# A feed-forward stage in seven block products, with the down product as a stage of its own

## The chip, the core and the metric

The kernel runs on one core of a Trainium2 chip. Times are device microseconds of one execution; the profile shows one execution more closely. Engines: PE (TensorE, matmuls), PEld (its weight loads), DVE (VectorE), ACT (ScalarE), POOL (GpSimd), and SP (SyncE), whose queue issues all DMAs here. Each engine runs its own instruction list in order; they wait for each other through semaphores.

## What is computed

Two transformer blocks on a sequence of 1024 rows of width 1024, all in float32. The part that is changed is the feed-forward layer of the first block (D_FF = 2816 = 22 x 128):

```
h2 = rms_norm(x, g_ffn[layer])
x = x + (jax.nn.silu(h2 @ w_ffn_gate[layer]) * (h2 @ w_ffn_up[layer])) @ w_ffn_down[layer]
```

The second block needs modulation vectors (shift, scale, gate), products of one activated row `c` with `ada_w_2` and `kv_ada_w_2`, 8192 columns in all: 64 pieces of 512 KB. They are computed beside the feed-forward layer.

## The kernel before, in words

Activations lie transposed: a tile holds 128 channels on the partitions and the 1024 rows of the sequence in the free dimension, in two halves (h = 0, 1) of 512. A float32 product is made of three fp32r matmuls: each operand is split in a high part and a low part (value minus high part), and high x high, high x low, low x high are summed in PSUM.

Weights come in units of 512 KB (128 x 1024 in SBUF). For each unit SP loads `raw` (`sp_w`), ACT makes the high part `wh` (`act_w`, L73), POOL the low part `wl` (`pool_w`, L76), PE uses it (`gemm`, L67). There are three places each for raw, high and low. `act_w(e, key, ahead)` is called at a fixed point of each engine's list and does all units up to so many past `key`.

The work runs as stages: attention and gates of the first block, branches, output product `out` (`pe_out`, by halves, with the squares and sums of the norm `n2`), feed-forward (`*_ffn`), a join with the last group of the down product (`*_join`), then the second block.

In the feed-forward stage hidden tile f (128 of 2816 columns) is a gate product `("fg", f)` and an up product `("fu", f)` on the tiles `bh`, `bl` (the scaled and split h2), 48 matmuls each. ACT takes silu of the gate, DVE multiplies by the up product (`hid`), ACT and POOL split the result in `G` (`gh`, `gl`), which holds five tiles. After each group of hidden tiles (GROUPS: 2, 4, 4, 4, 4, 4) `pe_down` adds the group before to the residual `X`: 8 products, DVE adds each to X. The last group is left to the join. The entry of the stage, `pe_first_two`, does half 0 of two products while the sums, root and scaling of half 1 are made.

The modulation runs between: per piece a DMA into `ada`, a DVE product and a DVE reduction (L106), and after every fourth piece four small matmuls. PSUM is four banks of 1024 columns, taken in turn (`take`).

Of the kernel before, what the change touches and what calls it, by code (L numbers as in the profile page):

```python
# [119 lines left out]
class Bank:  # L120


    def __init__(self, ap):
        self.ap, self.before = ap, []
# [12 lines left out]
class Net:  # L137
    def __init__(self, nc, A, C, out, mem, known, dry):
        self.nc, self.A, self.C, self.out, self.mem, self.dry = nc, A, C, out, mem, dry
        self.table, self.places, self.plan, self.unit_no = known  # L140
        self.sig = {}
        self.units = 0
# [29 lines left out]
    def setup(self):  # L172
        self.raw = [self.sb(f"raw{i}", i) for i in range(3)]
        self.wh = [self.sb(f"wh{i}", 3 + i, dt=FR) for i in range(3)]
        self.wl = [self.sb(f"wl{i}", 6 + i, dt=FR) for i in range(3)]
# [3 lines left out]
        self.banks = [Bank(t[:, :]) for t in self.mem["ps"]]  # L179
# [49 lines left out]
        self.X = [m(f"X{j}", 8 + j) for j in range(NT)]  # L229
        self.mh = [m(f"mh{j}", 16 + j, FR) for j in range(8)]  # L230
# [5 lines left out]
        self.ada = [m("ada0", 1), m("ada1", 7)]  # L236
        self.acc4 = self.sb("acc4", 51, 512)
# [18 lines left out]
        self.xs = self.dram("xs", [S, S])  # L256
        self.qd = self.dram("qd", [2048, S])
# [4 lines left out]
        self.n2 = five("n2", self.X)  # L262
        self.n3 = Norm("n3", self.X, t[0], t[1], half(t[3]), half(self.dg2), half(t[4]), t[2], self.v(V_GFIN))
        self.n4 = five("n4", self.X)
        self.n5 = five("n5", self.Y)

# [14 lines left out]
    def take(self, e, key, ring=None):  # L281
        ring = self.banks if ring is None else ring
        bank = ring.pop(0)
        ring.append(bank)
        for before in bank.before:
            e.wait_ge(*self.at("free", before))
        bank.before = [key]
        self.places[key] = bank.ap
        return bank.ap
# [4 lines left out]
    def part_banks(self):  # L294
        kept = self.banks.pop(0)
        self.kept = kept
        self.po = [Bank(kept.ap[:, 0:512]), Bank(kept.ap[:, 512:1024])]
        for x in self.po:
            x.before = list(kept.before)

    def join_banks(self):
        self.kept.before = self.po[0].before + self.po[1].before
        self.banks.insert(0, self.kept)
# [7 lines left out]
    def unit(self, key, w8):  # L311
        u = self.units
        self.units += 1
        if self.dry:
            self.plan.append(w8)
            self.unit_no[key] = u
        return u

    def upto(self, key, ahead):
        return min(self.unit_no[key] + ahead, len(self.plan)) if key is not None else ahead  # L320

    def sp_w(self, e, key, ahead=4):

        while self.n_sp < self.upto(key, ahead):
            u = self.n_sp
            src, nk, n = self.plan[u]
            if u >= 3:
                e.wait_ge(*self.at("whi", u - 3))
                e.wait_ge(*self.at("wlo", u - 3))
            e.dma_start(self.raw[u % 3][:, 0:nk * n].rearrange("p (k n) -> p k n", k=nk), src).then_inc(  # L330
                self.sig[f"raw{u % 3}"].up(("raw", u)), 16)
            self.n_sp += 1

    def act_w(self, e, key, ahead=3):
# [2171 lines left out]
```

## Time and profile before

| | us |
|---|---|
| median of 3 runs | 2804.19 |
| lowest, highest | 2799.44, 2804.88 |
| the profiled execution's own time | 2798.98 |
| its span, first to last instruction | 2797.4 |
| mean granted clock of TensorE | 0.976 of full speed |

The page gives for each engine the time in which it is busy; its slices and the windows show stretches. A wait of an engine is named by the instruction that ended it. The time of the profiled execution is its span and 1.6 us around it.

### The profile page before, as it was taken

The page shows a single profiled execution, that of the slowest core. Times are in us where ns is not written, and L with a number is a line of the kernel's source. Part 1 is how long each engine was busy: PE and PEld are TensorE (multiplying, and loading weights), DVE is VectorE, ACT ScalarE, POOL GpSimd, SP SyncE. Part 2 cuts the span into 40 slices and gives each one's busy share as a digit, 9 for nine tenths or more (in the row PEclk, how much of TensorE's full clock was granted, in tenths as well). Part 3 has the DMA queues.
Part 4 walks back from the last instruction along what each step waited for, and adds up shares of the span by engine and source line. Part 5 has one row for each costly group of instructions (what it writes and reads, how often), then busy time and mean ns, then how long its engine had stood idle before and what let it go on. Part 6 is the DMA issues. An engine that isn't in the chain of part 4 may idle for free. (4 is left out here: it accounts for less than half of the span.)

```text
span 2797.4 us, 30789 instructions
## 1 busy us (share of the span) xinstructions
PE 2647.7 (95%) x12448; PEld 2195.2 (78%) x12448; DVE 1420.0 (51%) x2330; ACT 858.6 (31%) x1307; POOL 941.0 (34%) x443
## 2 busy tenths in 40 slices
PE   5999999889998999999999978999999988999888
PEld 4888888678786888888888757888888866788877
DVE  5599999597425536364541273121313256007943
ACT  4432112477223211111111253212121245227732
POOL 2147422100544432333232334333242344323333
PEclk8999999999999999999999989999999989999999
DMA  4112233000542324343331111111111123332142
GB/s 159 43 38 61 91 91 99 26 1 31 181 136 76 113 75 121 106 121 99 112 105 51 48 53 46 45 50 41 50 48 45 53 68 106 121 104 67 50 143 98
DMA packets 292569, 221.78 MB, mean 79 GB/s; under 512 B 8425, under 2 KB 275149, under 8 KB 292429
## 3 DMA queue, kind: packets, MB, share of 16 engines
q1 hardware_dynamic: 292428, 219.82, 25.6%
q8 instruction: 99, 1.62, 0.2%
q14 instruction: 42, 0.34, 0.0%
HBM read 187.25 MB, written 31.49 MB: 78 GB/s over the span
## 5 line engine op out<-in xcount | busy, mean ns | idle before, releaser
L76 POOL TENSOR_TENSOR wl<-raw,wh 128x1024 fp32r<-128x1024 f32 (+1 forms) x226 | 560.5, 2483 | 824.2 <-ACT wh L73 821.2
L67 PE MATMUL ps<-bh,wh 128*128 128x512 f32 x1504 | 482.7, 395 | 23.2 <-POOL bl L76 9.9
L67 PE MATMUL ps<-bl,wh 128*128 128x512 f32 x1504 | 476.6, 391 | 0.0
L67 PE MATMUL ps<-bh,wl 128*128 128x512 f32 x1504 | 476.3, 391 | 0.0
L73 ACT ACTIVATE wh<-raw 128x1024 fp32r<-128x1024 f32 (+1 forms) x226 | 236.5, 1050 | 554.6 <-PE ps L67 498.4
L67 PEld LDWEIGHTS ps<-bh,wh 128*128 128x128 f32 x1504 | 283.5, 189 | 92.0 <-issue 17.7
L67 PEld LDWEIGHTS ps<-bh,wl 128*128 128x128 f32 x1504 | 284.0, 189 | 59.9
L67 PEld LDWEIGHTS ps<-bl,wh 128*128 128x128 f32 x1504 | 284.4, 189 | 59.1 <-issue 0.7
L76 POOL TENSOR_TENSOR gl<-tmp,gh 128x1024 fp32r<-128x1024 f32 x54 | 129.5, 2399 | 478.6 <-ACT gh L73 478.6
L73 ACT ACTIVATE tmp<-ps 128x1024 f32<-128x1024 f32 (+5 forms) x144 | 130.0, 905 | 454.8 <-PE ps L67 448.3
L67 PE MATMUL ps<-gh,wh 128*128 128x512 f32 x736 | 242.7, 397 | 15.1 <-POOL gl L76 6.9
L67 PE MATMUL ps<-gl,wh 128*128 128x512 f32 x736 | 239.9, 393 | 0.0
L67 PE MATMUL ps<-gh,wl 128*128 128x512 f32 x736 | 239.9, 393 | 0.0
L67 PE MATMUL ps<-ah,wh 128*128 128x512 f32 (+1 forms) x608 | 192.0, 393 | 14.3 <-DVE xt L85 9.8
L67 PE MATMUL ps<-al,wh 128*128 128x512 f32 (+1 forms) x608 | 190.7, 391 | 0.0
L67 PE MATMUL ps<-ah,wl 128*128 128x512 f32 (+1 forms) x608 | 190.5, 390 | 0.0
L67 PEld LDWEIGHTS ps<-gh,wh 128*128 128x128 f32 x736 | 139.4, 190 | 46.0 <-issue 8.6
L100 DVE MATCH_REPLACE8 sm<-m,sm 128x384 f32<-128x384 f32 (+2 forms) x192 | 166.1, 870 | 0.0
L73 ACT ACTIVATE gh<-tmp 128x1024 fp32r<-128x1024 f32 x54 | 57.3, 1061 | 351.1 <-DVE tmp L76 231.6
L67 PEld LDWEIGHTS ps<-gl,wh 128*128 128x128 f32 x736 | 140.1, 190 | 29.7 <-issue 0.5
L67 PEld LDWEIGHTS ps<-gh,wl 128*128 128x128 f32 x736 | 139.8, 190 | 29.6
L97 DVE MAX8 m<-sm 128x8 f32<-128x384 f32 (+2 forms) x192 | 160.4, 874 | 0.0
(188 smaller groups left out, 3991.2 us busy)
## 6 DMA issues: line engine op xcount, KB each, us to landing
ada<-in_ada_w SPq DMA_DIRECT2D x48, 512.0 KB, 3.8
raw<-in_w_in SPq DMA_DIRECT2D x37, 512.0 KB, 4.4
raw<-in_a_w_in SPq DMA_DIRECT2D x32, 512.0 KB, 3.9
raw<-in_w_ffn_down SPq DMA_DIRECT2D x26, 512.0 KB, 4.7
raw<-in_w_ffn_gate SPq DMA_DIRECT2D x22, 512.0 KB, 4.8
raw<-in_w_ffn_up SPq DMA_DIRECT2D x22, 512.0 KB, 4.9
raw<-in_a_w_out SPq DMA_DIRECT2D x20, 512.0 KB, 3.4
gates<-tmp SPq DMA_DIRECT2D x16, 512.0 KB, 3.0
```

The source lines that it names most:

```text
L67: return self.e.matmul(*a, **k) if self.e else Ins()
L73: return self.e.activation(*a, **k) if self.e else Ins()
L76: return self.e.tensor_tensor(*a, **k) if self.e else Ins()
L97: return self.e.max(*a, **k) if self.e else Ins()
L100: return self.e.match_replace(*a, **k) if self.e else Ins()
```

## The change

The gate and up products of a hidden tile are written as one product of 2 x 2 blocks: the columns are [gate, up], the inner dimension is cut in two (channels 0 to 511, 512 to 1023) and so are the rows of the sequence. With weight blocks A11 (gate, first channels), A12 (gate, other channels), A22 (up, other channels) and sums s1 to s4 of blocks, and activation blocks B11, B21, B22 and T1 to T4, seven block products P1, P2, P3, Q4, Q5, Q6, Q7 of 12 matmuls each stand in place of eight. POOL makes the weight sums (`pool_sum`); each sum and each block is split in a high and a low part. The activation blocks are made once, at the entry of the stage: half 0 by `*_set0` in the `out` stage, half 1 and the differences by `*_set1`. Four of the opening blocks (P1 and P2 of tiles 0 and 1) need half 0 only (`pe_begin`). Three of the products accumulate on a bank of PSUM after DVE (ACT for P2) has read what was there (`ONTO`), and DVE forms the four results with U and V (`dve_pair`).

The blocks need more of SBUF: X is spilled to DRAM (`xd`) in the `out` stage and read again at the end of the stage; hidden tiles are stored in DRAM (`hd`), and five groups of the down product follow as a stage of their own, reading them back into `tmp` (`sp_down`, `act_down`, `pool_down`). For tiles 2 to 19 there is a fourth raw place and three more places for weight blocks.

In all stages a unit of weights is now split in two blocks of 512 columns, with six places, so that `act_w` and `pool_w` work per block and `gemm` waits per block; PSUM is handed out in halves of 512 columns. The modulation is cut otherwise: a piece is 128 rows of 1024 columns (4 KB rows), DVE does one operation per piece (sum so far plus row times scalar), four pieces per tile in tiles 2 to 17, and eight small matmuls follow every eighth piece. The loads of X for the `out` stage all come after the last branch product.

```diff
+        self.B2 = self.seven("B2", {"B11": 8, "B21": 12, "T1": 16, "T2": 20, "T3": 24, "B22": 28, "T4": 32})
...
+    def pair(self, key, w0, w1, begun=False):
+
+        u = self.new_unit(key, w0)
+        v = self.new_unit(key, w1)
+        b0 = self.n_blocks
+        kinds = ("s1", "s2", "s3", "s4", "A22") if begun else ("A11", "s1", "s2", "s3", "A12", "s4", "A22")
+        at = {kind: b0 + i for i, kind in enumerate(kinds)}
+        for kind in kinds:
+            w, c = (u, 512 if kind == "A12" else 0) if kind[:2] in ("A1",) else (v, 512)
+            frees = (v,) if kind == "A22" else (u,) if kind == "s4" and begun or kind == "A12" else ()
+            self.new_block("w" if kind[0] == "A" else kind, w if kind[0] == "A" else u, c, pair=(u, v, at), frees=frees)
+        return u, at
+
...
+    def pool_sum(self, e, b):
+
+        kind, u, c, n, pair = self.blocks[b]
+        if kind == "w":
+            return
+        u, v, at = pair
+        r0, r1 = self.raw_of[u][1], self.raw_of[v][1]
+        low, high = slice(0, 512), slice(512, 1024)
+        for event in self.slot_free[b]:
+            e.wait_ge(*self.at(*event))
+        e.wait_ge(*self.at("raw", u))
+        e.wait_ge(*self.at("raw", v))
+        if kind in ("s2", "s4"):
+            e.wait_ge(*self.at("wsum", at[{"s2": "s1", "s4": "s2"}[kind]]))
+        x, y = {"s1": lambda: (r1[:, low], r1[:, high]), "s2": lambda: (r0[:, low], self.block_sum(at["s1"])),
+                "s3": lambda: (r0[:, low], r1[:, low]),
+                "s4": lambda: (r0[:, high], self.block_sum(at["s2"]))}[kind]()
+        e.tensor_tensor(self.block_sum(b), x, y, ALU.add).then_inc(self.sig["wlo"].up(("wsum", b)), 1)
+
...
+    def pool_w(self, e, key, ahead=6):
+
+        end = self.upto(key, ahead)
+        while self.n_pool < end:
+            b = self.n_pool
+            kind, u, c, n, pair = self.blocks[b]
+            need = b if kind not in ("s1", "s2") else pair[2][{"s1": "s2", "s2": "s4"}[kind]]
+            while self.n_sum <= need or self.n_sum <= min(b + 3, end - 1) and self.loaded_by(self.n_sum, b):
+                self.pool_sum(e, self.n_sum)
+                self.n_sum += 1
+            e.wait_ge(*self.at("bhi", b))
+            src = self.raw_of[u][1][:, c:c + n] if kind == "w" else self.block_sum(b)
+            e.tensor_tensor(self.block_lo(b)[:, 0:n], src, self.block_hi(b)[:, 0:n].bitcast(F32),
+                            ALU.subtract).then_inc(self.sig["wlo"].up(("blo", b)), 1)
...
+    SEVEN = {"P1": ("A11", "B11", "a"), "Q5": ("s1", "T1", "d"), "Q6": ("s2", "T2", "b"), "Q7": ("s3", "T3", "c"),
+             "P2": ("A12", "B21", "a"), "P3": ("s4", "B22", "d"), "Q4": ("A22", "T4", "c")}
+    ONTO = {"P2": "p1", "P3": "V", "Q4": "c22"}
...
+    def dve_pair(self, e, key, U, V, c12, c21, c22, free12=(), free2=(), hooks={}):
+
+        vec = self.sig["vec"]
+        b, c, d = (self.ps((key, x)) for x in "bcd")
+        e.wait_ge(*self.at("p1", key))
+        e.wait_ge(*self.at("prod", key, "Q6"))
+        e.tensor_tensor(U, U, b, ALU.subtract).then_inc(vec.up(("U", key), ("free", (key, "b"))), 1)
+        e.wait_ge(*self.at("U", key))
+        e.wait_ge(*self.at("prod", key, "Q5"))
+        e.tensor_tensor(V, U, d, ALU.add).then_inc(vec.up(("V", key)), 1)
+        e.wait_ge(*self.at("V", key))
+        e.wait_ge(*self.at("prod", key, "Q7"))
+        for event in free2:
+            e.wait_ge(*self.at(*event))
+        e.tensor_tensor(c22, V, c, ALU.add).then_inc(vec.up(("c22", key)), 1)
+        if "c22" in hooks:
+            hooks["c22"]()
+        e.wait_ge(*self.at("prod", key, "P3"))
+        for event in free12:
+            e.wait_ge(*self.at(*event))
+        e.tensor_tensor(c12, U, d, ALU.add).then_inc(vec.up(("c12", key), ("free", (key, "d"))), 1)
+        if "c12" in hooks:
+            hooks["c12"]()
+        e.wait_ge(*self.at("prod", key, "Q4"))
+        e.tensor_tensor(c21, U, c, ALU.add).then_inc(vec.up(("c21", key), ("free", (key, "c"))), 1)
...
+    def dve_set1(self, e, nm, B, g, after):
+
+        vec = self.sig["vec"]
+        x0, x1 = ([nm.X[j][:, h * 512:h * 512 + 512] for j in range(NT)] for h in (0, 1))
+        for i in range(4):
+            self.dve_scale(e, nm, i, 1, g, [("spilled", nm.name, 1, i)])
+        for event in after:
+            e.wait_ge(*self.at(*event))
+        for i in range(4):
+            e.wait_ge(*self.at("scaled", nm.name, 1, i))
+            e.tensor_tensor(B.f32["T1"][i], x0[i], x1[i], ALU.subtract).then_inc(vec.up(("set", B.name, "T1", i)), 1)
+        for i in range(4, NT):
+            self.dve_scale(e, nm, i, 1, g, [("spilled", nm.name, 1, i)])
+        for i in range(4):
+            e.wait_ge(*self.at("scaled", nm.name, 1, 4 + i))
+            e.wait_ge(*self.at("set", B.name, "T1", i))
+            e.tensor_tensor(x1[i], x1[4 + i], x1[i], ALU.subtract).then_inc(vec.up(("set", B.name, "T3", i)), 1)
+        for i in range(4):
+            e.wait_ge(*self.at("set", B.name, "T3", i))
+            e.tensor_tensor(B.f32["T2"][i], x0[i], x1[i], ALU.add).then_inc(vec.up(("set", B.name, "T2", i)), 1)
+            if i:
+                self.block_low(e, B, "T2", i - 1, B.f32["T2"][i - 1], self.sig["vlo"])
+        for i in range(4):
+            e.wait_ge(*self.at("D", B.name, i))
+            e.tensor_tensor(B.f32["T4"][i], B.f32["T4"][i], x1[i], ALU.add).then_inc(vec.up(("set", B.name, "T4", i)), 1)
+            block, k = ("T4", i - 1) if i else ("T2", 3)
+            self.block_low(e, B, block, k, B.f32[block][k], self.sig["vlo"])
+        self.block_low(e, B, "T4", 3, B.f32["T4"][3], self.sig["vlo"])
+
...
+        A, B = self.A, self.B2
+        ws = [[self.w8(A[name][0], 128 * f) for f in range(self.NF)] for name in ("w_ffn_gate", "w_ffn_up")]
+        self.pe_begin(e, [("ff", 0), ("ff", 1)], ws[0][:2], B, {
+            ("P1", 0): lambda: self.pe_sums(e, self.n2, 1), ("P1", 1): lambda: self.pe_rstd(e, self.n2, 1)})
+        for f in range(self.NF):
+            if f == 2:
+                self.add_raw("x", MAIN + 2, self.set_done(B))
+                for i in (3, 4, 5):
+                    self.add_slot(MAIN + i, self.set_done(B))
+            if f == 20:
+                self.drop("x", [MAIN + 3, MAIN + 4, MAIN + 5])
+            g = (f - self.ADA0) // 2 - 1
+            self.pe_pair(e, ("ff", f), ws[0][f], ws[1][f], B, f < 2,
+                         {"P1": lambda: self.pe_ada(e, g)} if 0 <= g < 8 and (f - self.ADA0) % 2 == 0 else {})
+        for g in range(5):
+            self.pe_down(e, "down", g, A["w_ffn_down"][0], 128 * self.group(g)[0], self.group(g),
+                         [self.GP[f] for f in self.group(g)])
+
...
+        self.sp_w(e, (("ff", 0), "begin"), 4)
+        for event in self.set_done(self.B2):
+            e.wait_ge(*self.at(*event))
+        for f in range(self.NF):
+            self.sp_w(e, ("ff", f), 4)
+            c = 4 * (f - self.ADA0)
+            if f == 2:
+                self.sp_ada(e, 0)
+                self.sp_ada(e, 1)
+            if 0 <= c < 64:
+                self.sp_ada(e, c + 2)
+                self.sp_ada(e, c + 3)
+            if f == 21:
+                self.sp_down(e, 1)
+            i = f % 2
+            e.wait_ge(*self.at("hid", f))
+            e.dma_start(self.hd[f * 128:f * 128 + 128, :], self.hidden_place(f)[1][:, :]).then_inc(
+                self.sig[f"st{i}"].up(("hstored", f)), 16)
+            if 0 <= c < 60:
+                self.sp_ada(e, c + 4)
+                self.sp_ada(e, c + 5)
+            if f == 20:
+                self.sp_down(e, 0)
+        for j in range(NT):
+            e.wait_ge(*self.at("prod", ("ff", 21), "P1" if j < 4 else "P2"))
+            e.dma_start(self.X[j][:, :], self.xd[j * 128:j * 128 + 128, :]).then_inc(
+                self.sig[f"xl{j}"].up(("x2", j)), 16)
+        self.sp_w(e, ("down", 0, "w", 0), 4)
+        for f in range(2, 6):
+            self.sp_down(e, f)
+        for g in range(5):
+            for j in self.down_units(g)[1]:
+                self.sp_w(e, ("down", g, "w", j), 4)
+            for f in self.group(g + 2) if g + 2 < 6 else ():
+                self.sp_down(e, f)
+
+    def sp_down(self, e, f):
+        i, free = self.down_place(f)
...
+        self.act_w(e, (("ff", 0), "begin"), 6)
         self.act_sums(e, self.n2, 1)
-        self.act_rstd(e, self.n2, 1)
-        self.act_scaled(e, self.n2, 1, 1, self.bh, after=[self.OUT_HALF[1]])
-        for f, done in self.hidden():
-            if f:
-                self.act_w(e, ("fg", f))
-                self.act_w(e, ("fu", f))
-            s = self.tmp[f % 5]
-            e.wait_ge(*self.at("prod", ("fg", f)))
-            if f < 5:
-                e.wait_ge(*self.at("nlo", "n2", 1, 1, 6))
-                e.wait_ge(*self.at("nlo", "n2", 1, 1, 7))
+        for f in (0, 1):
+            self.act_p1(e, ("ff", f), self.uv(f)[0], self.branch_over())
+            if f == 0:
+                self.act_rstd(e, self.n2, 1)
+        self.act_set1(e, self.n2, B, [self.OUT_HALF[1]])
+        e.wait_ge(*self.at("acc", "n2", 0, 1, 7))
+        for f in (0, 1):
+            self.act_silu(e, f)
+        for f in range(self.NF):
+            if f >= 2:
+                self.act_w(e, ("ff", f), 6)
+                self.act_p1(e, ("ff", f), self.uv(f)[0], self.set_done(B) if f < 4 else [("c21", ("ff", f - 2))])
+                if f == 21:
+                    self.act_down(e, 0)
+                self.act_w(e, ("ff", f), 10)
+                self.act_silu(e, f)
+                if f == 21:
+                    self.act_down(e, 1)
+                self.act_w(e, ("ff", f), 11)
...
+        self.pool_w(e, (("ff", 0), "begin"), 6)
+        self.pool_set1(e, self.n2, self.B2)
+        for f in range(self.NF):
+            if f == 21:
+                self.pool_w(e, ("ff", f), 3)
+                self.pool_down(e, 0)
+                self.pool_w(e, ("ff", f), 6)
+                self.pool_down(e, 1)
+            self.pool_w(e, ("ff", f), 13 if f < 20 else 7)
+        self.pool_w(e, ("down", 0, "w", 0))
+        for f in range(2, 6):
+            self.pool_down(e, f)
+        for g in range(5):
+            for j in self.down_units(g)[1]:
+                self.pool_w(e, ("down", g, "w", j))
+            for f in self.group(g + 2) if g + 2 < 6 else ():
+                self.pool_down(e, f)
```

## Rows read from the trace of the kernel before

**Rows 1.** The page: busy time, share of the span, instructions.

```profile
PE 2647.7 (95%) x12448; PEld 2195.2 (78%) x12448; DVE 1420.0 (51%) x2330; ACT 858.6 (31%) x1307; POOL 941.0 (34%) x443
```

**Rows 2.** Busy time by stretch: length, engines (instructions), PE clock, DMA share, GB/s.

```profile
900.00:940.00 40.00, 35.16 (x154) 27.53 (x153) 31.72 (x24) 11.05 (x14) 16.61 (x8) 1.00 0.31 90
...
940.00:1560.00 620.00, 620.00 (x2794) 515.14 (x2793) 262.31 (x190) 94.82 (x94) 193.74 (x75) 1.00 0.33 98
```

**Rows 3.** Timeline of DVE: start, length, instruction, idle before and releaser.

```profile
1565.08 1.22 DVE L76 TENSOR_TENSOR tmp<-tmp,ps 128x1024 f32<-128x1024 f32 x1 [20.54 <-PE ps L67]
...
1586.84 1.22 DVE L76 TENSOR_TENSOR tmp<-tmp,ps 128x1024 f32<-128x1024 f32 x1 [20.54 <-PE ps L67]
```

**Rows 4.** Waits of PE over the span: total, times, longest.

```profile
PE ps L67 <- POOL wl L76: 18.1, 5, 5.8
```

**Rows 5.** Timeline of PE, at two gaps.

```profile
864.25 0.39 PE L67 MATMUL ps<-mh,wl 128*128 128x512 f32 x1
870.48 0.76 PE L67 MATMUL ps<-mh,wh 128*128 128x512 f32 x1 [5.85 <-POOL wl L76]
871.04 0.63 PE L67 MATMUL ps<-ml,wh 128*128 128x512 f32 x1
871.47 0.63 PE L67 MATMUL ps<-mh,wl 128*128 128x512 f32 x1
...
1591.72 0.47 PE L67 MATMUL ps<-gh,wh 128*128 128x512 f32 x1 [2.94 <-POOL gl L76]
1592.02 0.39 PE L67 MATMUL ps<-gl,wh 128*128 128x512 f32 x1
```

**Rows 6.** Timeline of POOL and DVE, around 868 and 900 us.

```profile
866.76 1.28 POOL L76 TENSOR_TENSOR bl<-tmp,bh 128x512 fp32r<-128x512 f32 x1 [1.95 <-ACT bh L73]
...
867.99 5.15 POOL L76 TENSOR_TENSOR wl<-raw,wh 128x1024 fp32r<-128x1024 f32 x2
...
868.18 2.71 DVE L76 TENSOR_TENSOR tmp<-tmp,tmp 128x512 f32<-128x512 f32 x1 [0.77 <-ACT tmp L73]
...
900.10 1.29 POOL L76 TENSOR_TENSOR bl<-tmp,bh 128x512 fp32r<-128x512 f32 x1 [6.64 <-ACT bh L73]
```

**Rows 7.** Groups by form: busy, mean ns, idle before.

```profile
L76 DVE TENSOR_TENSOR X<-X,ps 128x512 f32<-128x512 f32 x32 | 21.8, 683 | 57.4 <-PE ps L67 57.4
```

**Rows 8.** Timeline of DVE and POOL, 1144 to 1150 us.

```profile
1146.47 1.52 DVE L76 TENSOR_TENSOR ada<-ada,cact 128x1024 f32<-128x1024 f32 x1
...
1146.88 3.39 POOL L76 TENSOR_TENSOR wl<-raw,wh 128x1024 fp32r<-128x1024 f32 x1
...
1148.03 2.03 DVE L106 TENSOR_REDUCE acc<-ada 128x128 f32<-128x1024 f32 x1
```

**Rows 9.** Timeline of DVE at the entry of the stage.

```profile
888.70 0.69 DVE L76 TENSOR_TENSOR X<-X,ps 128x512 f32<-128x512 f32 x1 [3.36 <-PE ps L67]
...
894.21 0.69 DVE L76 TENSOR_TENSOR tmp<-ident,r 128x512 f32<-128x512 f32 x1
...
897.94 1.42 DVE L79 SCALAR_TENSOR_TENSOR tmp<-X,vec,tmp 128x512 f32<-128x512 f32 x2 [3.04 <-ACT tmp L73]
...
900.07 2.53 DVE L79 SCALAR_TENSOR_TENSOR tmp<-X,vec,tmp 128x512 f32<-128x512 f32 x2
...
903.31 2.52 DVE L79 SCALAR_TENSOR_TENSOR tmp<-X,vec,tmp 128x512 f32<-128x512 f32 x2
```

**Rows 10.** Timeline of ACT at the entry of the stage.

```profile
897.30 0.60 ACT L73 ACTIVATE tmp<-ps 128x512 f32<-128x512 f32 x1 [3.34 <-PE ps L67]
...
912.22 1.28 ACT L73 ACT_TABLE_LOAD   x1 [2.49 <-POOL bl L76]
```

**Rows 11.** Stretches with 512 B packets (949) and 4 KB packets (2694).

```profile
949.00:954.00 5.00, 5.00 (x24) 4.14 (x23) 0.46 (x1) 1.63 (x2) 1.13 (x2) 1.00 1.04 304
...
2694.00:2699.00 5.00, 5.00 (x24) 4.14 (x23) 0.75 (x1) 0.00 (x0) 0.00 (x0) 1.00 1.03 415
```

**Rows 12.** Weight loads of 1000 to 1500 us, from issue to landing.

```profile
DMA to landing us min/median/max: 3.3/4.8/6.8
```

More of the change, by code:

```diff
@@ L178, in setup @@
             self.mem["ps"] = [self.nc.alloc_psum_tensor(f"ps{i}", [128, S], F32) for i in range(4)]
-        self.banks = [Bank(t[:, :]) for t in self.mem["ps"]]
+        self.halves = [Half(t[:, h * 512:h * 512 + 512]) for t in self.mem["ps"] for h in (0, 1)]
+        self.pool4, self.takes = [0, 1, 2, 3], 0
         o = [0]
@@ L265, in setup, with seven, parts @@
         self.n5 = five("n5", self.Y)
+    def seven(self, name, tiles):
+        def parts(i, off, dt, n):
+            return self.sb(f"{name}{n}{i}", MAIN + i, 512, dt, off)[:, :]
+        return Blocks(name, *({block: [parts(t + i, off, dt, n) for i in range(4)] for block, t in tiles.items()}
+                              for off, dt, n in ((0, FR, "h"), (2048, FR, "l"), (2048, F32, "s"))))
     def v(self, base):
@@ L277, in g12s, with take @@
         return self.g12[:, j:j + 1]
[L281 to L289, printed above, removed]
+    def take(self, e, key, wide=True, ring=None):
+        self.takes += 1
+        if ring is not None:
+            place = [ring.pop(0)]
+            ring.extend(place)
+        elif wide:
+            i = min(self.pool4, key=lambda i: max(h.taken for h in self.halves[2 * i:2 * i + 2]))
+            place = self.halves[2 * i:2 * i + 2]
+        else:
+            place = [min((self.halves[2 * i + h] for i in self.pool4 for h in (0, 1)), key=lambda x: x.taken)]
+        for half in place:
+            for before in half.before:
+                e.wait_ge(*self.at("free", before))
+            half.before, half.taken = [key], self.takes
+        self.places[key] = place[0].ap if len(place) == 1 else self.mem["ps"][i][:, :]
+        return self.places[key]
     def ps(self, key):
@@ new lines, in new_block @@
+    def new_block(self, kind, u, c=0, cols=512, pair=None, frees=()):
+        b = self.n_blocks
+        self.n_blocks += 1
+        place = self.slots.pop(0)
+        self.slots.append(place)
+        if self.dry:
+            self.slot_of.append(place[0][1])
+            self.slot_free.append(place[1])
+            self.blocks.append((kind, u, c, cols, pair))
+            self.first.setdefault(u, b)
+            for v in frees:
+                self.last[v] = b
+        place[1] = (("bused", b),)
+        return b
@@ L442, in pe_sums @@
     def pe_sums(self, e, nm, h):
-        p = self.take(e, ("sums", nm.name, h))
+        p = self.take(e, ("sums", nm.name, h), nm.two)
         for i in range(4):
```

581 lines of the change are left out of this document (338 added, 243 removed).

## The prediction

> **What bounds the kernel now.** I read the busy shares first: the tensor engine (PE) is busy 95% of the span, no other engine above 51% [rows 1]. Then busy time by stretch: from 940 to 1560 us PE has no idle time (VectorE, DVE, is busy 42%, GpSimd, POOL, 31%, DMA 0.33), and only the entry of the feed-forward stage loses, 4.84 of the 40 us after 900 [rows 2]. So here the time is the number of matmuls. The distance between two hidden products on DVE is 21.76 us for 96 matmuls, 0.2267 us each [rows 3]. The list of waits says who makes PE wait elsewhere: mostly POOL's low part of a weight tile, five times, 18.1 us [rows 4]; one stands at 870.48, and behind it matmuls start 0.43 us apart, not 0.23, for seven steps [rows 5]: a gap costs its length and about 1.5 us of slow clock. After the 2.94 us gap before 1591.72 the next start is 0.30 later [rows 5]: short gaps cost nothing extra.
>
> **Matmuls removed.** A hidden tile had 2 products of 8 x 3 x 2 = 96 matmuls; now 7 blocks of 4 x 3 = 84. 22 x 12 = 264, times 0.2267, is **-59.8 us**, all on the path, as PE has no idle time there. The rate stays if block changes are as free as tile changes; worse is a rival below. The 64 small modulation matmuls stay 64.
>
> **What is added per tile.** POOL made two low parts of 1024 columns; now 4 sums and 7 low parts of 512. One of 512 takes 1.28 us and the next starts 1.23 later [rows 6], so 11 x 1.25 = 13.8 us of a tile's 19.04 (84 x 0.2267). DVE gets five 512-wide sums out of PSUM, 0.68 each [rows 7], one 1024-wide product from SBUF, and four modulation steps of 1.22 in tiles 2 to 17 in place of 1.22 + 2.02 per old step. DVE and POOL take turns where both read SBUF: a DVE sum of 1.22 took 1.52 beside POOL, and POOL's 2.40 became 3.39 as it waited for that sum [rows 8]; two POOL operations of 2.35 took 5.15 with DVE's in between [rows 6]. So a 1024-wide DVE operation costs POOL about 1.0 and a 512-wide one 0.45. POOL with five such turns: 13.8 + 5 = 18.8, just below 19.04. ScalarE (ACT): ten halves of 0.6, hidden.
>
> **The entry.** Today: last update of the residual 888.70, diagonal 894.21, first scaling 897.94, then 3.24 us for three DVE operations and one of POOL [rows 9] (1.29 us, beginning 900.10 [rows 6]). After the change the sums run behind 12 matmuls, not 16 to 24, and the copy of the root, today 897.30 [rows 10], comes 1.7 earlier, so scaling starts at 896.25. To the last block, T4, DVE has 30 operations (8 scalings; 4 each for T1, T3, T2, T4; the low parts between): 30 x 0.69 = 20.7. POOL has 12 low parts and two sums meanwhile, all from SBUF: nearly each makes DVE wait (1.15 less overlap, 0.95): 13.3. T4 is whole at 930.3. On ACT stand behind it: its copy (0.65), the table load for silu (1.28, as at 912.22 [rows 10]), two silus (0.6 each), and only then the high part of weight sum s3 (0.6): 934.1; POOL's low part of s3 935.4. Q7 needs it. Then POOL looks ahead: before the low part of A22 it makes three sums for the next tile, which need that tile's second weight load, whose buffer comes free at 936.7; landing 3.4 later, 940.2; sums and low part to 945.3; Q4 ends 948.1. Without waits: 888.5 + 1.8 (sums, root) + 4 x 2.72 + 5 x 2.72 = 914.7 (four opening blocks, five of tile 0). Loss 33.4 against 4.84 today: **+28.6 us**. If DVE and POOL didn't wait for each other T4 would be there at 917 and Q4 end near 934: +15. If every turn cost its full length: +34.
> The Trainium skill (SBUF — State Buffer, SBUF: two separate sides) says that the pair of ports is locked for the full instruction. By this rule the 14 turns cost 1.29 each, 18.1, and the entry +33.4; the trace disagrees a little (5.15 for 2 x 2.35 plus 0.45).
>
> **The steady tiles.** POOL makes the sums s1 and s2 of tile f+2 before the low part of A22 of tile f+1. They need both weight loads of f+2. SP issues these after the store of hidden tile f and two modulation loads. The store waits for DVE: block Q4 of f ends (time 0), +0.2, c21 0.68, product 1.22, a turn 0.5: 2.5. Behind it lie 0.5 MB of store, 1 MB of modulation rows (4 KB pieces: 415 GB/s, 1.27 us a piece) and 1 MB of weights (512 B pieces: 304, 1.71) [rows 11]: 7.2 us, and some 1.8 until the first byte (a weight load lands 3.3 us after issue at the least [rows 12]). Landing: 11.6. Two sums, the low part, one turn: 3 x 1.29 + 1.0 = 16.5; Q4 of f+1 would start at 16.3. Then a sum and A11's low part with a turn (3.5): the next P1 at 20.0 where 19.0 was due. I take 0.9 us a tile; 15 tiles (3 to 17; before and after, no modulation loads stand ahead): **+13.5 us**. From below 0: a landing 1 us earlier; from above 2.5 a tile: landings go from 3.3 to 6.8 [rows 12].
>
> **Tile 21.** On ACT and POOL the first hidden tiles are read back inside it. Load 0 is issued behind store 20: lands at 7.2; ACT 1.06, POOL 2.4: 10.8; only then the low part of s3, 12.1, where Q7 was due at 8.2. Then tile 1: load after 10.8, ACT behind the silu of P2 (19), copy 20.1, POOL 22.6, and A22's low part behind it 23.9; Q4 was due at 20.2 and ends at 26.8, not 19.04: **+8 us** (2.5 if load 0 is early, 11 with the slow clock twice).
>
> **The down stage.** Same matmuls. The store of tile 21 goes at 2.2 after its Q4, then eight loads of X, two of weights, four hidden tiles: 0.5 MB each, on one queue. X ends at 15.4, weights 18.3, hidden 19.6 to 23.4 (at 415 GB/s). POOL needs 4 x 2.4 from 20.8: 30.3. Group 0 covers 96 x 0.2267 = 21.8; the first product of group 1 would end at 27.2 and ends at 31.7: 4.5 and a little clock, **+5.5 us** (0 to 12). Later groups: 43.5 us of PE against 20 of POOL and 4 MB, hidden. The Trainium skill (SBUF — State Buffer, A bandwidth-pool intuition that's wrong) gives HBM 358 GB/s a core; by it these loads end 3.3 us later and the sum is +9. The trace shows 415, so its rows are used.
>
> **What goes.** The stall of 2.94 for the last hidden tile [rows 5]: the last group's tiles are ready early, and what is late next is DVE in the join, as now: **-3.2**. Half-size weight blocks everywhere: a stall on POOL's low part ends 1.1 us sooner (2.4 to 1.28): four such, **-4** (between -8 and +3, for 226 more instructions on ACT and POOL, 0.2 each, mostly under PE). Spills of X, the loads of X moved behind the branches (eight, 10 us, under three finished weight tiles of 16), four more sums in set 0 (2.8 on DVE under 5.4 a tile): 0, up to +3 without that cover.
>
> **Sum:** -59.8 + 28.6 + 13.5 + 8 + 5.5 - 3.2 - 4 = -11.4 on the profiled execution of 2798.98 (span 2797.4 and 1.6 around it): 2787.6. That execution lies 5.2 below the median of the runs shown, so I say **2793 us**.
>
> **Rivals.**
> 1. Slower: the loads set the pace. Place: POOL's wait for the second weight load before A22's low part. Every us that it lands later costs one in 15 tiles; above 1.66 a tile the change is a loss. At 2.5: +24, **2817**. For it: 3.67 MB a tile in 19 us is 193 GB/s, against 98 now [rows 2], in a burst, with landings of 4.8 in the median [rows 12] where two loads follow each other. Against: the sum of piece times leaves me at 0.9.
> 2. Tiles run at PE's pace: loads land 1 us earlier. -13.5: **2779**. For it: no wait of PE between 940 and 1560 now; against: the reads ahead of A22, and POOL at 18.8 of 19.04.
> 3. The entry is cheap: DVE and POOL overlap, or the reads ahead find their buffer free. -14: **2779**. Against: the 3.24 us cycle.
> 4. The change doesn't bring its matmuls' time: each of 154 block changes (a new bank, two waits) costs 0.1 us on PE: +15, **2808**. Against: tile changes of the old kernel are free.
>
> **How the numbers follow.** Forecast 0.36, its own range 2782 to 2803; rival 1 0.27, rival 2 0.17, rival 3 0.10, rival 4 0.10. What this kernel's measurement can tell is 0.2%, 5.6 us: below 2798.6 is faster, above 2809.8 slower. Faster: 0.30 of the forecast + 0.17 + 0.10 = 0.57; same: 0.05 + 0.02 (rival 1) + 0.07 (rival 4) = 0.14; slower: 0.01 + 0.25 + 0.03 = 0.29. Range: down to rivals 2 and 3 with better blocks, 2766, up to rival 1 with a dear entry, 2822; outside are two of them together, 2 in 10.
>
> **What would show it.** 264 fewer 512-wide matmuls. PE's waits between 895 and 950: some 30 us, on DVE's and POOL's parts of the blocks, one on POOL ending near 935 and one near 945. In tiles 3 to 17 one wait per tile, PE on POOL's weight part, near 1 us; hidden products 20 us apart (19.04 by rival 2, 21.5 by rival 1), and 19.04 in tiles 18 to 20. In tile 21 two waits on POOL; one at group 1 of the down stage, releaser POOL's hidden low part. Wrong would be: no such wait, hidden products 21.8 apart (no gain in matmuls), or loss outside this stage.

## The result and the profile after

The changed kernel takes 2814.22 us (median of 5 runs, 2810.50 to 2817.16), the kernel before 2804.19 (2799.44 to 2805.92, 5 runs): ratio 1.0038, interval 1.0024 to 1.0053, slower by 10 us. The profiled executions differ by 11.5: 2810.5 against 2798.98. All terms below are read from these two.

Below are the page's engine line of the changed kernel and the two stretches of [rows 2] (stretch, length, PE, its weight loads, DVE, ACT, POOL, PE clock, DMA share, GB/s).

```profile
PE 2609.4 (93%) x12184; PEld 2153.3 (77%) x12184; DVE 1405.6 (50%) x2392; ACT 948.8 (34%) x1655; POOL 1221.4 (43%) x831
...
900.00:940.00 40.00, 18.58 (x54) 12.02 (x53) 34.89 (x34) 17.44 (x28) 25.70 (x16) 0.67 0.04 13
940.00:1560.00 620.00, 584.22 (x2579) 477.88 (x2578) 243.80 (x238) 162.57 (x263) 430.35 (x285) 0.99 0.45 150
```

The 264 matmuls are gone (12448 to 12184). PE, which had no idle time from 940 to 1560 [rows 2], now idles 36 us of those 620, and 21 of the 40 us ahead of them, where it had idled 4.84. POOL's work in the 620 us has grown from 194 to 430 us. Behind the stage the time did not change in these two traces: from the first update of the second block's residual (1800.38 before, 1811.75 after) to the end both take 997.0 us.

The starts of the hidden products on DVE give the time tile by tile. Below, in the timeline of DVE after, are those of tiles 0, 1, 2, 17, 18, 19, 20 and 21.

```profile
952.45 2.00 DVE L79 SCALAR_TENSOR_TENSOR tmp<-tmp,tmp 128x1024 f32<-128x1024 f32 x1
968.83 2.11 DVE L79 SCALAR_TENSOR_TENSOR tmp<-tmp,tmp 128x1024 f32<-128x1024 f32 x1
992.96 2.00 DVE L79 SCALAR_TENSOR_TENSOR tmp<-tmp,tmp 128x1024 f32<-128x1024 f32 x1
...
1312.14 1.82 DVE L79 SCALAR_TENSOR_TENSOR tmp<-tmp,tmp 128x1024 f32<-128x1024 f32 x1
1333.78 2.04 DVE L79 SCALAR_TENSOR_TENSOR tmp<-tmp,tmp 128x1024 f32<-128x1024 f32 x1
1352.81 2.26 DVE L79 SCALAR_TENSOR_TENSOR tmp<-tmp,tmp 128x1024 f32<-128x1024 f32 x1
1371.85 1.60 DVE L79 SCALAR_TENSOR_TENSOR tmp<-tmp,tmp 128x1024 f32<-128x1024 f32 x1
1402.00 1.23 DVE L79 SCALAR_TENSOR_TENSOR tmp<-tmp,tmp 128x1024 f32<-128x1024 f32 x1
```

Tiles 19 and 20 take 19.03 and 19.04: PE's own pace. Tile 21 takes 30.15. Tiles 3 to 17 take 319.18, which is 15 x 19.04, 7 groups of modulation matmuls on PE at 2.0, and **19.6 of stall**. Tile 1 has five blocks left at 952 (13.6 us) and takes 16.4, tile 2 takes 24.1 for 19.04: **7.9 more**.

The next rows are of one steady tile: SP's issues (the store of a hidden tile, two modulation loads, then two weight loads), POOL, and PE.

```profile
1207.85 0.33 SPq L109 DMA_DIRECT2D hd<-tmp  x1
1208.22 1.20 SPq L109 DMA_DIRECT2D ada<-in_ada_w  x2
1209.47 0.50 SPq L109 DMA_DIRECT2D raw<-in_w_ffn_gate  x1
1210.01 0.58 SPq L109 DMA_DIRECT2D raw<-in_w_ffn_up  x1
...
1211.42 1.30 POOL L76 TENSOR_TENSOR wl<-ws,wh 128x512 fp32r<-128x512 f32 x1
1218.67 1.28 POOL L76 TENSOR_TENSOR ws<-raw 128x512 f32<-128x512 f32 x1 [5.96 <-DMA raw<-in_w_ffn_up]
1220.10 2.10 POOL L76 TENSOR_TENSOR ws<-raw,ws 128x512 f32<-128x512 f32 x1
1222.15 1.27 POOL L76 TENSOR_TENSOR wl<-rawx,wh 128x512 fp32r<-128x512 f32 x1
...
1223.57 0.47 PE L67 MATMUL ps<-B2h,wh 128*128 128x512 f32 x1 [1.93 <-POOL wl L76]
```

POOL stands 5.96 us before two weight sums of the tile after next, until their load lands; the low part behind them, at 1222.15, is of data that had long been there, and PE waits 1.93 us for it. DVE's sums and products lie beside POOL's operations and stretch some of them (2.10 for 1.28).

The waits of PE at the entry, and those in tile 21 and at group 1 of the down stage:

```profile
908.21 0.47 PE L67 MATMUL ps<-B2h,wh 128*128 128x512 f32 x1 [1.40 <-POOL B2l L76]
922.32 0.77 PE L67 MATMUL ps<-B2h,wh 128*128 128x512 f32 x1 [8.12 <-DVE B2l L76]
925.66 0.77 PE L67 MATMUL ps<-B2h,wh 128*128 128x512 f32 x1 [1.73 <-DVE B2l L76]
...
938.10 0.77 PE L67 MATMUL ps<-B2h,wh 128*128 128x512 f32 x1 [6.19 <-ACT wh L73]
948.58 0.47 PE L67 MATMUL ps<-B2h,wh 128*128 128x512 f32 x1 [2.22 <-ACT wh L73]
...
1383.85 0.75 PE L67 MATMUL ps<-B2h,wh 128*128 128x512 f32 x1 [4.70 <-POOL wl L76]
1396.56 0.47 PE L67 MATMUL ps<-B2h,wh 128*128 128x512 f32 x1 [2.68 <-POOL wl L76]
1425.16 0.70 PE L67 MATMUL ps<-gp,wh 128*128 128x512 f32 x2 [2.26 <-ACT gp L73]
```

The last block of tile 0 starts at 948.58 and ends at 951.4; without waits it would have been 915.1: 36.3 us lost where 4.84 were before. The wait that ends at 938.10 is put down to ACT, but POOL's low part of s3, begun at 936.73, ended as late.

### The profile page after: what moved, and what is told of

Its sections match the earlier page's. It is cut to its first block, busy times and chain, and to the rows that moved or that the text cites. A ratio compares the mean times of both kernels' runs of the same rounds, so it can differ in the third digit from the quotient of the medians.

```text
span 2808.7 us, 31354 instructions
## 1 busy us (share of the span) xinstructions
PE 2609.4 (93%) x12184; PEld 2153.3 (77%) x12184; DVE 1405.6 (50%) x2392; ACT 948.8 (34%) x1655; POOL 1221.4 (43%) x831
## 4 chain that ended last, share of the span: by engine, by line
PE 63%; DVE 13%; POOL 9%; DMA 6%; ACT 6%; issue 2%; SPq 1%; POOLq 0%; DVEq 0%; ACTq 0%
PE ps L67 63%; POOL ws L76 4%; ACT tmp L73 3%; POOL wl L76 3%; DMA raw<-in_w_ffn_up 3%; DVE tmp L103 2%; DVE tmp L79 2%; DMA rawx<-in_w_ffn_up 2%; DVE ptl L79 1%; DVE p2l L76 1%; DVE tmp L76 1%; DVE XO L79 1%; SPq L109 1%; DVE st L82 1%; DMA tmp<-hd 1%
## 5 line engine op out<-in xcount | busy, mean ns | idle before, releaser
L76 POOL TENSOR_TENSOR wl<-raw,wh 128x512 fp32r<-128x512 f32 (+1 forms) x421 | 553.2, 1332 | 603.4 <-ACT wh L73 603.2
L73 ACT ACTIVATE wh<-raw 128x512 fp32r<-128x512 f32 (+1 forms) x421 | 246.5, 621 | 467.6 <-PE ps L67 274.3
L67 PE MATMUL ps<-B2h,wh 128*128 128x512 f32 x616 | 249.4, 405 | 52.8 <-POOL wl L76 25.0
L67 PE MATMUL ps<-bh,wh 128*128 128x512 f32 x800 | 263.6, 401 | 23.0 <-POOL bl L76 9.7
L67 PE MATMUL ps<-bl,wh 128*128 128x512 f32 x800 | 259.4, 396 | 0.0
L67 PE MATMUL ps<-bh,wl 128*128 128x512 f32 x800 | 259.2, 395 | 0.0
L67 PE MATMUL ps<-B2l,wh 128*128 128x512 f32 x616 | 244.7, 397 | 0.0
L67 PE MATMUL ps<-B2h,wl 128*128 128x512 f32 x616 | 244.5, 397 | 0.0
L67 PEld LDWEIGHTS ps<-bl,wh 128*128 128x128 f32 x800 | 153.6, 192 | 32.0 <-issue 0.5
L73 ACT ACTIVATE tmp<-tmp,st 128x128 f32<-128x128 f32 (+7 forms) x224 | 135.7, 607 | 52.0 <-DVE st L82 50.0
```

Source lines behind the costliest of these rows:

```text
L67: return self.e.matmul(*a, **k) if self.e else Ins()
L73: return self.e.activation(*a, **k) if self.e else Ins()
L76: return self.e.tensor_tensor(*a, **k) if self.e else Ins()
```

## The experiments

In all ten kernels the arithmetic is that of the changed kernel, except where it is said. Ratios are to the kernel before, run on the same chip, with a 95% interval. Gains in us are differences from the changed kernel's 2814.2 (ratio 1.0038, 1.0024 to 1.0053); the kernel before had medians from 2802.55 to 2804.19, so a gain of a few us is shown only where the intervals of the ratios lie apart.

**1. Loads two places earlier.** In tiles 1 to 17 SP issues the weight loads two units (one tile) sooner, ahead of the store of the hidden tile.

```
-            self.sp_w(e, ("ff", f), 4)
+            self.sp_w(e, ("ff", f), 6 if 1 <= f < 18 else 4)
```

> Edit: SP issues both weight loads of tile f+2 at the head of tile f (once the low parts of tile f are done), before the store of hidden tile f and the modulation loads, for f = 1 to 17. Theory A (the read-ahead sums on POOL wait for loads that are issued behind the hidden store): the waits of POOL on the second weight load in tiles 3 to 17 go (now some 5 us each), PE's 1.93 + 0.49 us waits per tile go, hidden products stand 19.04 us apart without and 21.0 with a group of modulation matmuls; 19.6 us in tiles 3 to 17 and some 3 in tile 2 are gained: 22 us below the changed kernel, 12 below the old one. Rival P (POOL, with 11 operations of 1.25 us and five turns with DVE, is the bound of a tile): the loads land early, the distances stay near 20.3, under 5 us gained. Rival D (the DMA queue is full, 193 GB/s a tile): the wait moves to the modulation loads and DVE, PE then waits on DVE's U and V; under 8 us gained.

Measured: 2797.84 (10 runs), ratio 0.9982 (0.9973 to 0.9991): 16 us off. The hidden products of tiles 2 and 18 on DVE:

```profile
995.22 1.98 DVE L79 SCALAR_TENSOR_TENSOR tmp<-tmp,tmp 128x1024 f32<-128x1024 f32 x1
...
1319.72 2.03 DVE L79 SCALAR_TENSOR_TENSOR tmp<-tmp,tmp 128x1024 f32<-128x1024 f32 x1
```

These 16 tiles (3 to 18) take 324.5 in place of 340.8, 16.3 less. Over PE's pace and eight modulation groups only 3.9 are left. So the stall needed the late loads; POOL's amount of work, which is the same, did not make it. I had expected 22: tile 2 came 2.3 later, not 3 earlier (see 7).

**2. No sums ahead.** The loads stay; POOL no longer forms the sums of a later tile before the low parts of this one.

```
-            while self.n_sum <= need or self.n_sum <= min(b + 3, end - 1) and self.loaded_by(self.n_sum, b):
+            while self.n_sum <= need:
```

> Edit: POOL makes a weight sum only when the low part at hand needs it, not up to three blocks ahead; the loads are issued as in the changed kernel. Theory A: A22's low part no longer stands behind two sums that wait for late loads; PE's wait before Q4 goes in tiles 3 to 17 (19.6 us) and in tile 0 (about 5 of the entry), and tile 1 and 2 gain 3 to 5: 25 to 30 us below the changed kernel, 15 to 20 below the old one. Rival L (the loads themselves are too late, in whatever order POOL works): PE then waits for A11 or s1 of the next tile instead, and under 8 us are gained. Rival P (POOL's throughput): no gain, distances of 20.3 stay.

Measured: 2793.76 (6 runs), ratio 0.9964 (0.9950 to 0.9978): 20 us off. POOL's waits for loads, from the lists of waits between 990 and 1330 (engine, us in total, times, longest), first after, then here:

```profile
POOL ws L76 <- DMA raw<-in_w_ffn_up: 39.2, 7, 11.0
POOL ws L76 <- DMA rawx<-in_w_ffn_up: 29.6, 8, 6.1
...
PE ps L67 <- POOL wl L76: 15.1, 14, 3.2
```

```profile
POOL ws L76 <- DMA raw<-in_w_ffn_up: 1.0, 1, 1.0
```

69 us of POOL standing for loads became 1, and PE's row for POOL is gone. ACT still waits 130.5 us for late loads of the other matrix, and in these tiles PE waits only for DVE, 6.5 us. With experiment 1: the time was lost where a late load and ready work behind it in POOL's queue came together; taking away either removes most of it (16.3 and 12.1 of 20.2 us). In this trace the product of tile 18 comes 20.4 us earlier: 2.6 at the entry, 5.8 in tiles 1 and 2, 12.1 in tiles 3 to 18. (Its execution took 2784.29, the least of the six; 5 us more were gained behind the stage.) I had expected 25 to 30, with all 19.6 of the steady tiles.

**3. Tile 21.** The parts of the first two hidden tiles, read back inside tile 21, are formed after its weight parts. The cut shows POOL's list; ACT's is changed likewise.

```
-            if f == 21:
-                self.pool_w(e, ("ff", f), 3)
-                self.pool_down(e, 0)
-                self.pool_w(e, ("ff", f), 6)
-                self.pool_down(e, 1)
             self.pool_w(e, ("ff", f), 13 if f < 20 else 7)
+        self.pool_down(e, 0)
+        self.pool_w(e, ("ff", 21), 11)
+        self.pool_down(e, 1)
```

> Edit: in tile 21 ACT and POOL make all weight parts of the tile first and the parts of hidden tiles 0 and 1 after them; the rest as in the changed kernel. Theory: the two waits of PE in tile 21 (4.70 and 2.68 us, with slow matmuls behind the first) go, the last two hidden products stand 19 to 20 us apart, not 30.2; group 0 of the down stage then waits up to 4 us for the part of hidden tile 1: 6 to 9 us below the changed kernel. Rival (what waits there is the reload from DRAM, wherever it stands): the same 11 us appear before group 0, no gain.

Measured: 2804.74 (11 runs), ratio 1.0007 (0.9998 to 1.0016): 9.5 off. Tile 21 takes 19.04 (1376.65 to 1395.69), 11.1 less, so the rival (the reload costs the same wherever it stands) falls; PE's waits there are gone, and one of 1.95 for a hidden low part, right behind, takes a part back:

```profile
1398.15 0.70 PE L67 MATMUL ps<-gp,wh 128*128 128x512 f32 x2 [1.95 <-POOL gq L76]
```

**4. Half-size blocks alone.** The feed-forward stage of before (eight products, hidden tiles kept on chip, its modulation and its loads of X), with the weight blocks of 512 columns in six places and PSUM in halves.

> Edit: the old feed-forward stage (eight products, down product between, modulation and loads of X as before) on the new base: weight blocks of 512 columns in six places, PSUM in halves. It is the part of the change that touches all stages, alone. My prediction gave it -4 us; the trace after the change shows the stages outside the feed-forward 1 us shorter. Expected: 0 to -4 against the old kernel (2800 to 2804). Rival H (the loss of the change comes from halved blocks, with 226 more instructions on ACT and POOL each): +8 to +12, near the changed kernel's 2814.

Measured: 2794.54 (6 runs), ratio 0.9974 (0.9963 to 0.9985): 7.3 us, by the interval 4 to 10, below the kernel before (by medians on this chip 9.0). So this part of the change pays by itself, and the rest, the new stage with its modulation and loads, costs 20 against this kernel (18 by the ratios).

**5. Low parts of the entry on DVE.** Twelve low parts (T1, T3, B22) move from POOL to DVE; the cut leaves out the lines for T1.

```
-        for block in ("T1", "T3", "B22"):
-            for i in range(4):
...
-                self.block_low(e, B, block, i, src, self.sig["plo"])
+            self.block_low(e, B, "T3", i, x1[i], self.sig["vlo"])
+            self.block_low(e, B, "B22", i, x1[4 + i], self.sig["vlo"])
```

> The twelve low parts of the second half of the columns that POOL forms at the entry (blocks T1, T3, B22) move to VectorE. In the trace after, VectorE and POOL work beside each other from 906.9 to 933.1 us and both are slow: a VectorE addition takes 1.75 us beside POOL and 0.69 alone, a POOL one 1.66. Theory T (the two take turns, so the sum of their work sets the end): VectorE has 36 operations in place of 24, at 0.72 us each these take 26 us, as the 24 do now; the last block is whole at the same time within 2 us, and the kernel stays within 4 us of the changed one (2814). Rival V (VectorE's own count sets the end, POOL's is hidden): 12 more operations at 0.69 us, the entry 8 us later, 2822. Rival P (POOL's slow low parts are what TensorE waits for): the waits of TensorE for POOL's B2l (0.8 us each) go and the first silu comes 3 to 6 us earlier, 2809.

Measured: 2808.49 (10 runs), ratio 1.0025 (1.0016 to 1.0035): 5.7 off by medians, 3.6 by the ratios, whose intervals overlap, so the time alone does not show the gain; the traces show what became of the entry. The same kind of operation on DVE, after and here:

```profile
920.42 1.75 DVE L76 TENSOR_TENSOR B2l<-B2s,B2h 128x512 fp32r<-128x512 f32 x1
922.09 1.75 DVE L76 TENSOR_TENSOR B2s<-XO 128x512 f32<-128x512 f32 x1
923.76 1.75 DVE L76 TENSOR_TENSOR B2l<-B2s,B2h 128x512 fp32r<-128x512 f32 x1
```

```profile
920.21 0.68 DVE L76 TENSOR_TENSOR B2s<-B2s,XO 128x512 f32<-128x512 f32 x1
920.81 0.68 DVE L76 TENSOR_TENSOR B2l<-B2s,B2h 128x512 fp32r<-128x512 f32 x1
921.41 0.68 DVE L76 TENSOR_TENSOR B2l<-XO,B2h 128x512 fp32r<-128x512 f32 x1
```

From the first scaling to the last low part DVE had 32 operations in 33.7 us (900.77 to 934.47) and has 44 in 27.7 (900.46 to 928.11). Alone they start 0.60 apart, beside POOL 1.68. At the mean of the 44, 0.63 each, the 32 take 20.1, so the turns cost about 13.6. My theory T, that the last block would be whole at the same time within 2 us, fails: it is so 6 us earlier. It was right that the two take turns, but counted 0.72 for each operation. Rival P's signs came out: PE's waits for POOL's `B2l` are gone and the product of tile 0 comes 5.4 earlier (947.09). Rival V falls.

**6. ACT's order at the entry.** The root is taken before the high parts of the sums of tile 0; the high parts of s3, s4 and A22 before the silus.

```
-        self.act_w(e, (("ff", 0), "begin"), 6)
+        self.act_w(e, (("ff", 0), "begin"), 4)
         self.act_sums(e, self.n2, 1)
...
+        self.act_w(e, (("ff", 0), "begin"), 6)
         self.act_set1(e, self.n2, B, [self.OUT_HALF[1]])
+        self.act_w(e, ("ff", 0), 5)
```

> Only ScalarE's order at the entry changes: the root of the second half's norms is taken before the high parts of the weight sums of tile 0 (now it stands behind them, and they wait for a load that lands at 894.0 us), and the high parts of s3, s4 and A22 are formed before the first silus. Theory: the scale r is ready 4.7 us earlier (892.8 in place of 897.6), the whole chain behind it moves by that, and the wait of TensorE for s3 at 938.1 us (6.2 us) shrinks by some 2.5 more: 5 to 8 us off, 2806 to 2809. Rival (the weight sums of tile 0 on POOL, and the turns that VectorE and POOL take, set the entry, and the root only waits beside them): less than 2 us, 2812 to 2814.

Measured: 2811.65 (6 runs), ratio 1.0038 (1.0023 to 1.0053): nothing that can be told, as the rival had it. The first eight operations on DVE after, and here:

```profile
900.77 3.76 DVE L79 SCALAR_TENSOR_TENSOR XO<-XO,vec,tmp 128x512 f32<-128x512 f32 x4 [2.25 <-ACT tmp L73]
904.45 2.48 DVE L76 TENSOR_TENSOR B2s<-XO 128x512 f32<-128x512 f32 x4
```

```profile
895.88 4.81 DVE L79 SCALAR_TENSOR_TENSOR XO<-XO,vec,tmp 128x512 f32<-128x512 f32 x4 [3.04 <-ACT tmp L73]
900.61 6.78 DVE L76 TENSOR_TENSOR B2s<-XO 128x512 f32<-128x512 f32 x4
```

The chain starts 4.9 us earlier, about 1 of it because this execution was ahead already, and the eight operations take 11.5 in place of 6.2: POOL's weight sums, which begin when their load lands (893.2 here), now lie beside them. The rest of the gain, 2.6 at tile 0, is gone by tile 3 (1014.23 against 1013.62), where the loads set the pace.

**7. Both cures of the sums.** Edits 1 and 2 together.

> Both cures of the late sums together: the loads of a tile two places earlier, and no weight sums formed ahead of need on POOL. Theory (one cause: POOL's sums stand in its queue before a load that has not landed): the gains overlap in tiles 3 to 17, which then run at 20.3 us each, as with the earlier loads alone (16 us); what the second cure alone took off before tile 3 (8 us) is added: 24 us below the changed kernel, 2790. Rival (two separate waits, each with its own cost): 16 and 20 add up, 2778.

Measured: 2793.34 (5 runs), ratio 0.9969 (0.9957 to 0.9981): 21 off, no better than edit 2 alone. The gains overlap, as one cause has it, and the rival (16 and 20 add up, 2778) falls; of the 8 us before tile 3 none came (tile 2 at 992.99, after 992.96). SP and PE there:

```profile
971.63 0.37 SPq L109 DMA_DIRECT2D raw<-in_w_ffn_gate  x1
974.12 0.37 SPq L109 DMA_DIRECT2D raw<-in_w_ffn_up  x1
974.54 9.02 SPq L109 DMA_DIRECT2D ada<-in_ada_w  x4
...
984.58 0.80 PE L67 MATMUL ps<-B2h,wh 128*128 128x512 f32 x1 [6.92 <-DVE pv L76]
```

The weight loads that tile 2 now issues ahead (those of tile 4) stand on SP until 971.6, when their buffer comes free. The first modulation loads stand behind them and go at 974.54; with edit 2 alone they went at 967.14. DVE waits for them with its sums out of PSUM behind, and PE waits 6.92 us (1.80 with edit 2 alone).

**8. Four edits.** 1, 2, 3 and 6 together.

> Four edits together: earlier loads, no sums ahead, tile 21 without the parts of the hidden tiles in its middle, and ScalarE's order at the entry. From the 2790 that I expect of the first two, 9.5 less for tile 21 as measured alone, and 5 to 8 less for the entry: 2773 to 2776, some 28 us or 1% below the kernel before. Rival (the waits stand in for each other, so that a later one takes over): not below 2785.

Measured: 2776.48 (4 runs), ratio 0.9911 (0.9898 to 0.9923), at the upper end of what was expected; the rival (not below 2785) falls. Beside edits 1 and 2, edit 6 brings the product of tile 0 5.3 earlier (950.62 in kernel 7, 945.35 here).

**9. Early loads from tile 3 on, with edits 2 and 3**, the entry as it was: the condition reads `3 <= f < 18`.

> No sums ahead, tile 21 without the parts of the hidden tiles in its middle, and the earlier loads only from tile 3 on; the entry stays as it was. With the earlier loads from tile 1 the loads of the modulation matrices stood behind a weight load that waited for its buffer to come free (971.6 to 974.5 us), and TensorE waited 6.9 us for VectorE at 984.6. Theory: that goes, the hidden product of tile 2 is at 984.6 as with the sums alone changed, tiles 3 to 18 take the 20.3 us each of the earlier loads, so tile 18 is at 1309; with 9.5 for tile 21 the time is some 30 us below the changed kernel, 2784. Rival (the earlier loads of tile 3 collide with the modulation loads in any place): no better than the two cures from tile 1 on with tile 21's gain, 2784 in the median but tile 2 or 3 later than 992 or 1012 us.

Measured: 2779.09 (5 runs), ratio 0.9914 (0.9900 to 0.9927), 5 below what was expected. Tile 2 at 985.4 and tile 18 at 1310.9 on DVE: the theory within 2 us. Moving one condition by two tiles brought tile 2's product from 993.0 in kernel 7 to 985.4. It lacks edit 6 and is as fast as kernel 8 (the intervals overlap): kernel 8 is 3.9 ahead at tile 0 (945.35 against 949.20) and 2.2 behind at tile 2 (987.58).

**10. The same with both edits of the entry** (5 and 6).

> The same with both edits of the entry: the root first, and the twelve low parts of the second half on VectorE. Alone they brought 1 and 6 us, while the loads of tiles 1 to 3 stood behind them. Theory (the entry is a chain, its gains add once the loads no longer set the first tiles): root 4.9 us and turns 4.2 us, 8 to 9 us below the kernel without them, 2774 to 2776, and under the 2776.5 of the four edits. Rival (the first tiles take it back, whatever the entry does): within 3 us of the kernel without them.

Measured: **2763.55** (4 runs, 2762.42 to 2766.93), ratio 0.9858 (0.9845 to 0.9872): 51 us below the changed kernel and 40 below the one before. The stretches of [rows 2] now:

```profile
900.00:940.00 40.00, 23.31 (x71) 15.98 (x70) 30.86 (x46) 18.62 (x30) 14.16 (x11) 0.70 0.09 27
940.00:1560.00 620.00, 609.13 (x2728) 502.01 (x2727) 264.17 (x242) 162.86 (x267) 444.14 (x288) 1.00 0.46 152
```

Against kernel 9 it is 15.5 faster, where 8 to 9 were expected, so the rival (within 3 us) falls. In the traces the products come 9.0 earlier in tile 0 and 10.0 in tile 21, and the second block 11.3. The other 4 lie behind that, in code that is the same in both: that stretch took 991.2 us here, 995.2 in kernel 9, and 991.2 to 998.6 over all twelve traces. So 9 to 11 us are shown to be the entry's, and the rest is not shown to be of these edits. At tile 0 the two edits gave 2.6 and 5.4 alone and give 9.0 together, near their sum; what edit 6 lost again alone is kept here.

## Why the prediction was wrong

Forecast: -11.4 on the profiled execution; measured: +11.5. The step that failed is the condition of the late sums: I put tiles 1 and 2 at nothing, where 7.9 us were lost, and took the stall behind it at 0.9 us a tile, where it was 1.3. These two turn the sign (14.6 us with tile 18); the mechanisms were otherwise those forecast. Term by term, forecast and measured from the trace after:

- Matmuls: -59.8 and -59.8. Tiles 19 and 20 run at 19.03 and 19.04; rival 4 falls.
- Entry: +28.6 and +31.5; rival 3 falls. The turns were about right (13.3 said, 13.6 by experiment 5; the 30 operations to T4 took 32.3, where 34.0 were said). A detail that failed was the root: I moved ACT's copy 1.7 earlier, from 897.30 to 895.6, and had scaling start at 896.25. It started at 900.77, as ACT's root stood behind high parts of sums that wait for a load landing at 894.06, behind the spill on SP. I had not counted the DMA ahead of the moved step. T4 was whole at 933.1 for 930.3, and Q7 began at 938.10 for 935.4. Experiment 6 shows that this delay by itself cost little: POOL's sums lay in the way instead. The Trainium skill (SBUF — State Buffer, SBUF: two separate sides) has the pair of ports locked for the full instruction, by my count of 14 turns an estimate of 18.1; the traces again give less, 13.6.
- Tiles 1 and 2: 0 and **+7.9**. This is the largest single miss. I wrote "15 tiles (3 to 17; before and after, no modulation loads stand ahead)", so I made the modulation loads the condition of the stall, and tiles 1 and 2 free. But the sums ahead wait there too (2.55 us of PE in tile 1), and in tile 2 DVE waits for the first modulation load with PE's accumulators behind it (3.4). Experiment 2 takes 5.8 of the 7.9 away.
- Steady tiles: +13.5 and +19.6, and 0.6 in tile 18. The mechanism was the one forecast, shown twice (experiments 1 and 2, by different edits); the size was 1.3 a tile, not 0.9. Rival 2, no stall, falls. The second weight load is issued 2.16 us behind the store and POOL goes on 8.66 later: 10.8, where I had 9.1 from the store to the landing (my own pieces add to 9.0: 7.2 and 1.8). Rival 1 named the same place but needed 1.66 a tile to turn the sign by itself.
- Tile 21: +8 and +11.1, both waits where forecast, 4.70 and 2.68. The matmuls at half clock behind them (see below) cost 3.4 more, which I had as the case of 11. Down stage: +5.5 and +5.3; by my own 1.71 a load the weights behind X would end at 18.8, not the 18.3 that I wrote; ACT took them at 17.8. The Trainium skill (SBUF — State Buffer, A bandwidth-pool intuition that's wrong) gives HBM 358 GB/s a core, by which the estimate was +9. The trace does not agree: it shows 411 GB/s from 1420 to 1426, near the 415 that I used. Join: -3.2 and -3.2. Modulation matmuls: 0 and -2 (8 groups of 2.0 for 16 of 1.13).
- Half-size blocks outside the stage: -4 and 0 in this one trace; -7.3 by the ratio in experiment 4, -9.0 by its medians. The stretch from the first update of the second block to the end took 991.2 to 998.6 us in the twelve traces, though its code is the same in eleven of them (all but the kernel before), so a single trace can't give a term of 4 and the runs decide: it is negative and was, if anything, too small. Why the changed kernel's trace does not show it stays open, and so does why that stretch varies.

The measured terms add to 11.0. The forecast missed by 23 us, made up of many errors with one sign: 8 in tiles 1 and 2, 7 in the steady tiles, 3 each in the entry and tile 21, 4 outside, less 2 on the modulation. Entry, steady tiles and tile 21 each came out above my value but inside the bounds that I had given them (15 to 34, 0 to 2.5 a tile, 2.5 to 11). A saving of 60 against costs of 56, with 7 more saved elsewhere, had no room for errors that all go one way. The range, up to 2822, did hold the time.

Where the 60 us went can be read from the trace: entry 31, tiles 1 to 18 28, tile 21 11, down stage 5. The trace of kernel 10 has 12 of the 31, 21 of the 28 and all 11 back. That order and placing were to blame is shown for these 44; for the other 19 at the entry and the 5 of the down stage only the waits are known. Kernel 10 lies 51 us below the changed kernel with the same products.

## What to carry to other kernels

Work formed ahead of need on an in-order engine is a cost, not a cushion, if its input may be late: what stands behind it is ready and waits too. Price it in every tile in which it is issued, the first ones as well. When a load is moved forward, ask what stands behind it on its queue while it waits for its buffer (7 us here). And before a costed stage is given up, reorder: the same products went from 10 us slower to 40 us faster than the kernel before. The fair rival is the old stage with the half-size blocks (experiment 4): against it the seven products went from 20 slower to 31 faster.

## What the runs showed of the hardware

- DVE and POOL, both working in SBUF, come near to taking turns: DVE additions of 128x512 start 0.60 us apart alone and 1.68 beside POOL, whose own take 1.66 in place of 1.25. One of each thus takes 1.68, and one after the other would take 1.85. With POOL's twelve given to DVE the last low part was ready 6 us earlier.
- TensorE's granted clock was 1.00 (2.4 GHz) from 908 to 914. Then PE stood for 8.12 us, and from 922.5 the clock was 0.50 (1.2 GHz) and stayed there through the gaps of 1.73, 1.74 and 6.19 us. The matmuls from 938.10 start 0.43 apart for twelve of them, and from 944, at 1.00, 0.23 apart: those twelve cost 2.5 us more than at the full clock. Behind the gap of 4.70 in tile 21 seven start 0.39 to 0.54 apart from 1383.85 on. Behind the one of 2.68 four start at the full rate and then seven 0.43 apart, with a granted clock of 0.51 from 1397.5 to 1401. Behind gaps of 1.93 (1223.57) and 2.22 (948.58) the starts stay near 0.23.
- A 512 KB weight load of 512 B pieces lands 8.2 us after its issue in the steady tiles (median; 7.5 into the other buffer), with the store and modulation rows on the queue, where the median had been 4.8 and the least 3.3 [rows 12].
